# Three reorderings in a two-block transformer kernel on one core: sums of squares behind both chains, values' transposes ahead of the last tiles, output weights in idle buffers

## The chip, the cores and the metric

The kernel runs on one core of one Trainium2 chip. The metric is the device time of one launch in microseconds (us). PE is the matmul engine, DVE the vector engine, ACT the scalar engine, POOL GpSimd, SP the engine that issues the weights' DMAs. "PE waits for X" means that PE's next matmul needed a semaphore that X's last instruction raised.

## What is computed

512 tokens of width 1024 pass through two blocks of two layers each, all in float32. The first block's layer is feed-forward, token mixer, feed-forward; the second's, on 16 meta tokens and the 512, is token mixer, feed-forward. Cut to what matters:

```python
def first_block(x, ...):                       # per layer l
    x = x + 0.5 * rmsnorm(swiglu(rmsnorm(x, g1), w_gate, w_up, w_down), g2)
    x = x + rmsnorm(token_mixing(rmsnorm(x, g3), w_in, ..., w_out), g4)
    x = x + 0.5 * rmsnorm(swiglu(rmsnorm(x, g5), ...), g6)

def second_block(x, meta, ...):                # per layer l
    z = rms_norm(h, pre_g) @ w_in              # q, k, v, forget logits, conv parts
    y = concat([forgetting_attention(q, k, v, log_f), y_conv, y_sc])
    h = h + rms_norm(head_rms_norm(y, head_g) @ w_out, post_g)
    u = causal_depthwise_conv(rms_norm(h, g) @ w_up, conv_w)
    h = h + rms_norm((silu(gate) * up) @ w_down, post_g)
```

The first block's mixer ("mixer 1", M1) has three kinds of attention heads, of which one (stick-breaking) needs cumulative sums; the second's ("mixer 2", M2) is attention with a forget gate beside two convolutions.

## The kernel before, in words

**Stages.** The kernel is ten stages in a row, in the order F1 M1 F1 F1 M1 F1 M2 F2 M2 F2 (F for feed-forward, the digit for the block). Activations lie transposed: `x` is 128 partitions by 8 column groups by tokens. An edge is what lies between two stages: the last output columns of one, the residual sum, and the norm of the next. Tokens are cut into two halves h = 0 and 1 of about 256, so that an edge's work on one half runs beside matmuls of the other.

**Split floats.** Float32 products are made of three matmuls of a faster type: hi by hi, lo by hi, hi by lo. Weights come by DMA into two raw buffers, in granules of 128 x 1024 (512 KB). ACT writes a granule's hi part (`split_hi`, L589), DVE or POOL its lo part, raw minus hi (`split_lo`, L596; POOL in the mixers, DVE in the feed-forward stages). A "tile" is the three matmuls L605 to L607 or L646 to L648 (once for each half of the tokens where a stage has halves). `xhi`/`xlo` are the same parts of `x` (ACT L750, DVE L763). Each raw buffer is loaded again once both parts of its granule are made.

**An edge.** Each engine runs its own program in order; semaphores tie them. For each half, `dve_edge` scales the output (L851), adds it to `x` (L859), makes `xlo` (L763), and at the end `dve_x_sum` adds up the squares of the new `x` (L775, L777), which ACT has written into `y` (`act_x_square`, L755). Half 1's chain comes behind half 0's sum. `pe_first` runs the first three granules of the next stage piece by piece as `xhi`/`xlo` come; `pe_pre_sum` (L668) turns the DVE sum into the sum over all 1024 columns by one matmul, and ACT makes the norm factor `r` from it (L732, L734). `r` is applied to the outputs of the matmuls, so matmuls need only `xhi` and `xlo`, not `r`.

**Mixers.** In M1 and M2 PE walks through a list of steps: scores of one unit, transposes of the probabilities of an earlier one (`ptrans`), their product with the values (`pv`), and between them three parts of projection tiles (`st.parts`, `fill`) that need nothing of the attention. Some steps end with `vtrans`: four or five transposes of the values into PSUM, which ACT copies to `m_v` (L1542 in M1, L2103 in M2). The next step begins with a transpose into the same PSUM bank, which waits for that copy.

**The end of M2.** Output weights are 8 granules (OUT+0 to OUT+7; `OUT2_ORDER`, `omm`), for four pairs of output columns m = 0 to 3. m = 0 and 1 use the working buffers `whi`/`wlo`, m = 2 and 3 (`LATE`) buffers of their own (`m_late`). ACT's `act_out` makes the hi parts and moves the finished sums out of PSUM (`act_yevac`, L809 and L813); m = 3 of the matmuls waits for the PSUM banks of m = 1 (L646 waits for L813).

Of the kernel before, what the change touches and what calls it, by code (L numbers as in the profile page):

```python
# [316 lines left out]
def program(nc, I, out):  # L317
    with ExitStack() as ctx:
# [746 lines left out]

        def act_out(act, b, g, gb, gb2, qs, first=2):
# [5 lines left out]
            def hi_split(j):  # L1072
                m, q = divmod(j, nq)
                into = home(g, m, q)[0]
                n = qs[q] * PAIR
                if m not in LATE[g]:
                    split_hi(act, b, gb + j, gb2 + j // 2, j % 2, n)
                    return
                if KIND[g][0] == "F":
                    act.wait_ge(b.s.granules_done, gb + nq * late + {0: -1, 1: 0, 2: 1, 3: 1, 4: 2, 5: 2}[q] + CR)  # L1080
                elif m == late and q == 0:
                    act.wait_ge(b.s.pv_done, (LAYER[g] + 1) * (UNITS1 if b.n == 1 else UNITS2))
                split_hi(act, b, gb + j, gb2 + j // 2, j % 2, n, into)
# [1560 lines left out]
```

## Time and profile before

| what | value |
|---|---|
| median of 3 runs | 3505.8 us (3505.73 to 3506.83) |
| the profiled execution | 3504.3 us, its span 3502.6 us |
| granted clock of PE, mean | 0.992 of full |
| PE busy | 3376.0 us, 96% of the span |
| DVE, ACT, POOL busy | 1743.6, 1415.1, 312.5 us |

The span is the profiled part of the execution; 1.7 us of it lie around it. The busy time of PE is the modelled time of its matmuls, so that what is left for a schedule to win is PE's waits and the stretches at half clock.

### The profile page before, as it was taken

What the parts mean: (1) busy time and instruction counts of PE and PEld (TensorE: products, weight loads), DVE (VectorE), ACT (ScalarE), POOL (GpSimd) and SP (SyncE); (2) the same over time, 40 slices, a digit from 0 to 9 for tenths busy, and PEclk for the clock granted to TensorE, in tenths of its full rate; (3) what the DMA queues carried; (4) which work ended last, traced back from release to release, by engine and by line L of the source; (5) the groups of instructions that cost most, each with busy time, mean ns of one, the idle gap of its engine ahead of it and who ended that gap; (6) DMA issues with size and microseconds to landing.
All of it is one profiled execution on the core that took longest, in us unless ns stands there. A gap on an engine that the chain in (4) does not pass through costs nothing.

```text
span 3502.6 us, 52761 instructions
## 1 busy us (share of the span) xinstructions
PE 3376.0 (96%) x21254; PEld 2941.2 (84%) x21254; DVE 1743.6 (50%) x2382; ACT 1415.1 (40%) x2394; POOL 312.5 (9%) x167
## 2 busy tenths in 40 slices
PE   8999999899999999999899999988999999899998
PEld 7887866788888888866788889878999988789998
DVE  5442556544425442556544426735665366356643
ACT  4322445433234322445433234565443344644332
POOL 0000122100000000122000002210000022100000
PEclk9999999999999999999999999999999999999999
DMA  4343311233332332321233332212222321122222
GB/s 120 91 128 96 100 55 55 61 87 93 93 106 79 96 96 90 97 59 51 61 90 96 93 100 67 55 40 73 90 90 93 100 61 46 43 78 91 90 90 85
DMA packets 330446, 287.45 MB, mean 82 GB/s; under 512 B 9665, under 2 KB 326169, under 8 KB 330293
## 3 DMA queue, kind: packets, MB, share of 16 engines
q1 hardware_dynamic: 329348, 283.90, 27.2%
q8 instruction: 114, 1.87, 0.2%
q10 hardware_dynamic: 945, 1.37, 0.1%
q14 instruction: 39, 0.32, 0.0%
HBM read 283.10 MB, written 5.27 MB: 82 GB/s over the span
## 4 chain that ended last, share of the span: by engine, by line
PE 88%; DVE 5%; ACT 4%; issue 1%; DMA 1%; SPq 0%; ACTq 0%; DVEq 0%
PE ps L605 21%; PE ps L606 21%; PE ps L607 21%; PE ps L646 3%; PE ps L647 3%; PE ps L648 3%; PE ps L1783 2%; PE ps L1785 1%; PE ps L1784 1%; PE ps L698 1%; PE ps L1376 1%; PE ps L1400 1%; PE ps L1415 1%; PE ps L702 1%; PE ps L1832 1%
## 5 line engine op out<-in xcount | busy, mean ns | idle before, releaser
L605 PE MATMUL ps<-xhi,whi 128*128 128x512 f32 (+2 forms) x3088 | 1064.0, 345 | 4.1 <-DVE m_aconv L2170 4.0
L606 PE MATMUL ps<-xlo,whi 128*128 128x512 f32 (+2 forms) x3088 | 1057.3, 342 | 0.0
L607 PE MATMUL ps<-xhi,wlo 128*128 128x512 f32 (+2 forms) x3088 | 1053.1, 341 | 0.0
L596 DVE TENSOR_TENSOR wlo<-raw,whi 128x1024 fp32r<-128x1024 f32 x404 | 487.6, 1207 | 1114.3 <-ACT whi L589 1111.8
L589 ACT ACTIVATE whi<-raw 128x1024 fp32r<-128x1024 f32 (+1 forms) x495 | 515.4, 1041 | 1177.8 <-PE ps L607 1063.4
L605 PEld LDWEIGHTS ps<-xhi,whi 128*128 128x128 f32 x3088 | 583.4, 189 | 91.4 <-issue 19.0
L607 PEld LDWEIGHTS ps<-xhi,wlo 128*128 128x128 f32 x3088 | 582.4, 189 | 69.7
L606 PEld LDWEIGHTS ps<-xlo,whi 128*128 128x128 f32 x3088 | 582.9, 189 | 66.3 <-issue 0.5
L605 PE MATMUL ps<-hhi,whi 128*128 128x512 f32 (+2 forms) x1056 | 359.0, 340 | 0.9 <-issue 0.9
L606 PE MATMUL ps<-hlo,whi 128*128 128x512 f32 (+2 forms) x1056 | 358.1, 339 | 0.0
L607 PE MATMUL ps<-hhi,wlo 128*128 128x512 f32 (+2 forms) x1056 | 357.8, 339 | 0.0
L596 POOL TENSOR_TENSOR wlo<-raw,whi 128x1024 fp32r<-128x1024 f32 (+1 forms) x91 | 229.2, 2519 | 775.4 <-ACT whi L589 775.4
L782 POOL TENSOR_TENSOR S<-S 128x512 f32<-128x512 f32 (+5 forms) x58 | 77.8, 1341 | 2332.0 <-ACT S L809 2280.8
L605 PEld LDWEIGHTS ps<-hhi,whi 128*128 128x128 f32 x1056 | 198.9, 188 | 26.0 <-issue 2.7
L607 PEld LDWEIGHTS ps<-hhi,wlo 128*128 128x128 f32 x1056 | 198.6, 188 | 24.4
L606 PEld LDWEIGHTS ps<-hlo,whi 128*128 128x128 f32 x1056 | 198.9, 188 | 22.8
L1783 PE MATMUL ps<-xhi,whi 128*128 128x264 f32 x480 | 143.1, 298 | 1.9 <-DVE m_vt L2170 1.1
L1163 DVE SCALAR_TENSOR_TENSOR S<-S,par 128x528 f32<-128x528 f32 (+1 forms) x176 | 126.3, 759 | 24.1 <-ACT S L1027 18.2
L1043 ACT ACTIVATE hhi<-S 128x512 f32 (+4 forms) x132 | 82.3, 636 | 135.1 <-DVE S L1202 135.1
L1785 PE MATMUL ps<-xhi,wlo 128*128 128x264 f32 x480 | 136.3, 284 | 0.0
L1784 PE MATMUL ps<-xlo,whi 128*128 128x264 f32 x480 | 136.2, 284 | 0.0
L1035 ACT ACTIVATE S<-S 128x512 f32<-128x512 f32 (+2 forms) x132 | 82.0, 636 | 115.4 <-DVE S L1178 75.8
(274 smaller groups left out, 5150.9 us busy)
## 6 DMA issues: line engine op xcount, KB each, us to landing
raw<-in_ffn_w_up_dram SPq DMA_DIRECT2D x176, 512.0 KB, 3.7
raw<-in_ffn_w_down_dram SPq DMA_DIRECT2D x120, 512.0 KB, 3.4
raw<-in_w_in_dram SPq DMA_DIRECT2D x94, 512.0 KB, 3.8
raw<-in_ffn_w_gate_dram SPq DMA_DIRECT2D x88, 512.0 KB, 3.7
raw<-in_w_out_dram SPq DMA_DIRECT2D x32, 512.0 KB, 3.4
raw<-in_ffn_w_down_dram SPq DMA_DIRECT2D x24, 256.0 KB, 2.7
tbias_scratch<-rev_scratch SPq DMA_DIRECT2D x1, 3072.0 KB
y<-tbias_scratch SPq DMA_DIRECT2D x6, 512.0 KB, 6.1
```

Of the source, the lines that this page charges most:

```text
L589: act.activation(into[:, 0:n], raw[slot][:, 0:n], ACT.Copy).then_inc(b.s.weights_hi, 1)
L596: eng.tensor_tensor(lo[:, 0:n], raw[slot][:, 0:n], hi[:, 0:n].bitcast(F32), ALU.subtract).then_inc(b.s.weights_split, 1)
L605: pe.matmul(o, wh, hi[:, t0:t0 + w], start=first, stop=False)
L606: pe.matmul(o, wh, lo[:, t0:t0 + w], start=False, stop=False)
L607: ins = pe.matmul(o, wl, hi[:, t0:t0 + w], start=False, stop=last)
L646: pe.matmul(o, wh, hi, start=first, stop=False)
L647: pe.matmul(o, wh, lo, start=False, stop=False)
L648: return pe.matmul(o, wl, hi, start=False, stop=last)
L1163: ins = dve.scalar_tensor_tensor(out=c_, in0=S[o][:, k:k + b.T], scalar=tap(l, k, 2 * i + o, up), in1=c_, op0=ALU.mult, op1=ALU.add)
L1783: pe.matmul(o, wh, xhi[:, t, t0:t0 + w], start=(t == 0), stop=False)
L1784: pe.matmul(o, wh, xlo[:, t, t0:t0 + w], start=False, stop=False)
L1785: ins = pe.matmul(o, wl, xhi[:, t, t0:t0 + w], start=False, stop=(t == 7))
```

## The change

It has three parts, which share no semaphore and can be read one by one.

1. **Sums behind both chains.** In `dve_edge` the two calls of `dve_x_sum` stand behind both halves' chains. ACT's last squares stand one `xhi` later. In `pe_first` the two `pe_pre_sum` stand behind the first and the second half of granule 2's tiles of h = 1. Where more tiles of the stage's start follow (F2's `rest`, M2's fourth granule), each half waits for its own norm.
2. **Values' transposes ahead of the last tiles.** In steps with a `vtrans`, M1 and M2 call it before `fill(st.parts[2])` and not behind it. M1's step 0 runs all its tiles ahead of its scores.
3. **Output weights of m = 1 in idle buffers.** OUT+2 is split into `whi[2]`/`wlo[2]` in step 20 and OUT+3 into `ahi`/`alo` (a convolution's, free by then) in step 21, by ACT and DVE; OUT+4 and OUT+5 ahead of m = 0's evacuation. The output tiles k = 1 and 2 of m = 0 move from behind the steps into steps 21 and 22. `m_late` of M2 moves to another place in memory.

```diff
+OUT_STEP = {20: 2, 21: 3}
...
-    steps[21].parts = [[], [], [("o", 0, 6), ("o", 1, 6)]]
-    steps[22].parts = [[], [("o", 0, 4), ("o", 1, 4)], [("o", 0, 5), ("o", 1, 5)]]
+    steps[21].parts = [[], [("o", 0, 1), ("o", 1, 1)], [("o", 0, 6), ("o", 1, 6)]]
+    steps[22].parts = [[("o", 0, 2), ("o", 1, 2)], [("o", 0, 4), ("o", 1, 4)], [("o", 0, 5), ("o", 1, 5)]]
...
         def home(g, m, q):
+            if KIND[g] == "M2" and m == 1:
+                if q == 0:
+                    return whi[2], wlo[2]
+                return [t[:, :, :].rearrange("p a t -> p (a t)")[:, 0:1024] for t in (m2.ahi, m2.alo)]
...
-                else:
-                    pe_pre_sum(pe, g, 0)
                 half = len(tiles[2]) // 2
                 for t in tiles[2][:half]:
                     tile(h, 2, t)
                 if h == 1:
-                    pe_pre_sum(pe, g, 1)
+                    pe_pre_sum(pe, g, 0)
                 for t in tiles[2][half:]:
                     ins = tile(h, 2, t)
-            if rest:
-                pe.wait_ge(e.norm_log, pre(g, 1))
+                if h == 1:
+                    pe_pre_sum(pe, g, 1)
+            for h in range(2):
+                if rest:
+                    pe.wait_ge(e.norm_log, pre(g, h))
                 for t in rest:
-                    for h in range(2):
-                        ins = tile(h, 2, t)
+                    ins = tile(h, 2, t)
...
                 if nxt is not None:
                     dve_x_lo(dve, g + 1, nxt, h, 3)
+            if nxt is not None:
+                for h in range(2):
                     dve_x_sum(dve, g + 1, h, ch)
...
+        def out_hi(act, b, g, gb, gb2, qs, j):
+            nq, late = len(qs), LATE[g][0]
+            m, q = divmod(j, nq)
+            into = home(g, m, q)[0]
+            n = qs[q] * PAIR
+            if m not in LATE[g] and not (KIND[g] == "M2" and m == 1):
+                split_hi(act, b, gb + j, gb2 + j // 2, j % 2, n)
+                return
+            if KIND[g][0] == "F":
+                act.wait_ge(b.s.granules_done, gb + nq * late + {0: -1, 1: 0, 2: 1, 3: 1, 4: 2, 5: 2}[q] + CR)
+            elif m == 1:
+                act.wait_ge(b.s.granules_done, gb - (1 - q) + CR)
+            elif m == late and q == 0:
+                act.wait_ge(b.s.pv_done, (LAYER[g] + 1) * (UNITS1 if b.n == 1 else UNITS2))
+            split_hi(act, b, gb + j, gb2 + j // 2, j % 2, n, into)
...
+                if j == 0 and KIND[g] == "M2":
+                    for i in range(nq * late, nq * late + 2):
+                        hi_split(i)
                 if j == nq * late - 1 and KIND[g][0] == "M":
-                    for i in range(nq * late, nq * DOWN_PAIRS):
+                    for i in range(nq * late + (2 if KIND[g] == "M2" else 0), nq * DOWN_PAIRS):
                         hi_split(i)
                     next_hi(0)
...
-                fill(st.parts[2])
                 if st.vt is not None:
                     vtrans(st.vt)
+                if st.sc != 0:
+                    fill(st.parts[2])
...
+                if n_step in OUT_STEP:
+                    out_hi(act, b, sub, g2b(l) + OUT2, g2b2(l) + OUT2 // 2, OUT_Q, OUT_STEP[n_step])
...
-            for k in (1, 2):
-                for o in range(2):
-                    otile(o, k)
```

**DVE at an edge.** DVE's rows of the edge into the first mixer, before: the sum of half 0 (rows two to four) stands between half 0's last `xlo` and half 1's chain.

```order
L763 SCALAR_TENSOR_TENSOR xlo<-x,par,xhi 128x256 x4
L775 TENSOR_TENSOR y<-y 128x4x256
L775 TENSOR_TENSOR y<-y 128x2x256
L777 TENSOR_TENSOR y<-y 128x256
L851 SCALAR_TENSOR_TENSOR S<-y,S 128x512
L859 TENSOR_TENSOR x<-x,S 128x2x256
L851 SCALAR_TENSOR_TENSOR S<-y,S 128x512
```

The same place after the change:

```order
L768 SCALAR_TENSOR_TENSOR xlo<-x,par,xhi 128x256 x2
L864 TENSOR_TENSOR x<-x,S 128x2x256
L768 SCALAR_TENSOR_TENSOR xlo<-x,par,xhi 128x256 x4
L780 TENSOR_TENSOR y<-y 128x4x256
L780 TENSOR_TENSOR y<-y 128x2x256
L782 TENSOR_TENSOR y<-y 128x256
L780 TENSOR_TENSOR y<-y 128x4x256
L780 TENSOR_TENSOR y<-y 128x2x256
L782 TENSOR_TENSOR y<-y 128x256
```

The six sum rows now stand together behind the last `xlo`, ahead of nothing but the stage's own work; half 1's first L856 (L851 of before) follows directly on half 0's last `xlo`.

**PE at a values' transpose.** PE's rows at the end of an M1 step with `vtrans` (`m_vt`), before: all tiles, then the transposes, then the next step's first transpose (`m_w`) into the same bank.

```order
L607 MATMUL ps<-xhi,wlo 128x512
L605 MATMUL ps<-xhi,whi 128x512
L606 MATMUL ps<-xlo,whi 128x512
L607 MATMUL ps<-xhi,wlo 128x512
L1391 MATMUL ps<-ident,m_vt 128x128 x4
L1400 MATMUL ps<-ident,m_w 128x128
L1376 MATMUL ps<-m_k,m_q 128x384 x2
```

And after:

```order
L1410 MATMUL ps<-ident,m_vt 128x128 x4
L605 MATMUL ps<-xhi,whi 128x512
L606 MATMUL ps<-xlo,whi 128x512
L607 MATMUL ps<-xhi,wlo 128x512
L605 MATMUL ps<-xhi,whi 128x512
L606 MATMUL ps<-xlo,whi 128x512
L607 MATMUL ps<-xhi,wlo 128x512
L1419 MATMUL ps<-ident,m_w 128x128
```

Two tiles (six matmuls) now stand between the transposes of the values and the next transpose.

**ACT at the end of M2.** ACT's rows from the head norm's last operation to the evacuation of m = 1, before; the first row of L589 is OUT+2 and OUT+3.

```order
L2077 ACTIVATE m_ohi<-y,par 128x528
L589 ACTIVATE whi<-raw 128x1024 x2
L809 ACTIVATE S<-ps 128x528 x2
L813 ACTIVATE y<-ps,par 128x528 x2
L1093 ACT_TABLE_LOAD
L589 ACTIVATE m_late<-raw 128x1024 x4
L589 ACTIVATE whi<-raw 128x1024
L809 ACTIVATE S<-ps 128x528 x2
L813 ACTIVATE y<-ps,par 128x528 x2
```

And after (`m_ahi` stood in step 21, some rows ahead of this piece, `whi[2]` in step 20):

```order
L2105 ACTIVATE m_ohi<-y,par 128x528
L590 ACTIVATE m_late<-raw 128x1024 x2
L814 ACTIVATE S<-ps 128x528 x2
L818 ACTIVATE y<-ps,par 128x528 x2
L1107 ACT_TABLE_LOAD
L590 ACTIVATE m_late<-raw 128x1024 x2
L590 ACTIVATE whi<-raw 128x1024
L814 ACTIVATE S<-ps 128x528 x2
L818 ACTIVATE y<-ps,par 128x528 x2
```

Between the two evacuations (L809/L813, now L814/L818) stand two late splits and one of the next stage, where there were four and one; ahead of the first stand the other two.

## Rows read from the trace of the kernel before

**Rows 1.** The page, part 1, busy time of PE.
```profile
PE 3376.0 (96%) x21254; PEld 2941.2 (84%) x21254; DVE 1743.6 (50%) x2382; ACT 1415.1 (40%) x2394; POOL 312.5 (9%) x167
```

**Rows 2.** The waits of PE: us in total, times, longest.
```profile
PE ps L1400 <- ACT m_v L1542: 12.6, 16, 0.9
...
PE ps L1870 <- ACT m_v L2103: 7.4, 8, 0.9
...
PE ps L605 <- DVE m_aconv L2170: 4.0, 2, 2.0
```

**Rows 3.** The timeline of PE into the first mixer: start, us, what, [idle before].
```profile
402.62 0.36 PE L698 MATMUL ps<-xhi,whi 128*128 128x256 f32 x1 [1.20 <-ACT xhi L750]
...
411.56 0.59 PE L668 MATMUL ps<-y,ones 128*128 128x256 f32 x2
...
413.63 0.50 PE L605 MATMUL ps<-xhi,whi 128*128 128x512 f32 x1
```

**Rows 4.** The waits of PE at that edge, 400 to 414 us.
```profile
PE ps L702 <- DVE xlo L763: 0.8, 2, 0.5
```

**Rows 5.** The timeline of ACT at the same edge.
```profile
396.30 0.42 ACT L734 ACTIVATE S<-S 128x256 f32<-128x256 f32 x1
```

**Rows 6.** The timeline of DVE at the same edge.
```profile
399.78 0.43 DVE L777 TENSOR_TENSOR y<-y 128x256 f32<-128x256 f32 x1
400.12 0.69 DVE L851 SCALAR_TENSOR_TENSOR S<-y,S 128x512 f32<-128x512 f32 x1
...
408.63 1.95 DVE L775 TENSOR_TENSOR y<-y 128x1024 f32<-128x1024 f32 x2
```

**Rows 7.** The timeline of POOL at the same edge.
```profile
411.18 2.40 POOL L596 TENSOR_TENSOR wlo<-raw,whi 128x1024 fp32r<-128x1024 f32 x1 [47.11 <-ACT whi L589]
```

**Rows 8.** DVE beside POOL in mixer 2, first alone, then overlapped.
```profile
2218.07 2.12 DVE L2219 SCALAR_TENSOR_TENSOR m_aconv<-m_apad,par,m_aconv 128x528 f32<-128x528 f32 x3
...
2221.99 2.42 DVE L2219 SCALAR_TENSOR_TENSOR m_aconv<-m_apad,par,m_aconv 128x528 f32<-128x528 f32 x2
```

**Rows 9.** The timeline of POOL in the same stretch.
```profile
2220.77 2.40 POOL L596 TENSOR_TENSOR wlo<-raw,whi 128x1024 fp32r<-128x1024 f32 x1 [14.09 <-ACT whi L589]
```

**Rows 10.** The timeline of DVE, edge from mixer 1 to feed-forward.
```profile
708.52 1.23 DVE L596 TENSOR_TENSOR wlo<-raw,whi 128x1024 fp32r<-128x1024 f32 x1
```

**Rows 11.** PE at the same edge, first matmul of the last granule there.
```profile
710.85 0.28 PE L646 MATMUL ps<-xhi,whi 128*128 128x256 f32 x1
```

**Rows 12.** PE at the edge from mixer 2 to feed-forward.
```profile
2420.01 0.56 PE L698 MATMUL ps<-xhi,whi 128*128 128x264 f32 x1 [2.62 <-ACT xhi L750]
```

**Rows 13.** PE at the values' transposes of unit 4, mixer 1.
```profile
449.76 0.39 PE L607 MATMUL ps<-xhi,wlo 128*128 128x512 f32 x1
449.99 0.60 PE L1391 MATMUL ps<-ident,m_vt 128*128 128x128 f32 x4
451.37 0.30 PE L1400 MATMUL ps<-ident,m_w 128*128 128x128 f32 x1 [0.78 <-ACT m_v L1542]
```

**Rows 14.** ACT at the values' transposes of unit 24, mixer 1.
```profile
596.40 0.60 ACT L1485 ACTIVATE m_pt<-ps 128x512 f32<-128x512 f32 x1 [0.17 <-ACT m_w L1516]
```

**Rows 15.** The waits of PE, 2345 to 2390 us, end of mixer 2.
```profile
PE ps L646 <- ACT y L813: 5.5, 1, 5.5
PE ps L605 <- DVE wlo L596: 3.4, 2, 2.5
PE ps L605 <- DVE m_olo L2273: 1.6, 1, 1.6
```

**Rows 16.** ACT at the end of mixer 2.
```profile
2384.07 1.06 ACT L589 ACTIVATE whi<-raw 128x1024 fp32r<-128x1024 f32 x1 [2.81 <-DMA raw<-in_ffn_w_up_dram]
...
2386.01 1.29 ACT L813 ACTIVATE y<-ps,par 128x528 f32<-128x528 f32 x2
```

**Rows 17.** Windows: PE, PEld, DVE, ACT, POOL busy, granted clock, DMA share, GB/s.
```profile
2385.45:2392.28 6.83, 4.92 (x22) 4.92 (x23) 3.88 (x3) 5.05 (x10) 3.71 (x3) 0.50 0.39 117
2143.10:2146.50 3.40, 3.40 (x18) 3.40 (x17) 1.57 (x2) 0.00 (x0) 0.30 (x1) 0.50 0.78 222
```

More of the change, by code:

```diff
@@ L1072, in hi_split @@
             def hi_split(j):
[L1073 to L1083, printed above, removed]
+                out_hi(act, b, g, gb, gb2, qs, j)
             def next_hi(j):
@@ L1130, in act_out @@
                 act_x_square(act, g + 1, 0, p)
-            for p in range(4):
+            act_x_hi(act, g + 1, nxt, 1, 0)
+            for p in range(1, 4):
                 act_x_hi(act, g + 1, nxt, 1, p)
-                act_x_square(act, g + 1, 1, p)
+                act_x_square(act, g + 1, 1, p - 1)
+            act_x_square(act, g + 1, 1, 3)
         def first_hi(act, g, j):
@@ L1433, in pe_mix1 @@
                 if st.sc == 0:
-                    fill(st.parts[0])
+                    for part in st.parts:
+                        fill(part)
                 if st.sc is not None:
@@ L1442, in pe_mix1 @@
                     ptrans(u, 1)
-                fill(st.parts[1])
+                if st.sc != 0:
+                    fill(st.parts[1])
                 if st.extra is not None:
                     norm_sums(0)
-                fill(st.parts[2])
                 if st.vt is not None:
                     vtrans(st.vt)
+                if st.sc != 0:
+                    fill(st.parts[2])
                 if st.extra is not None:
@@ L1536, in act_mix1 @@
                     outputs(p_)
-                for g in st.done_in[1] + st.done_in[2]:
+                for g in st.done_in[1]:
                     if g < 24:
@@ L1543, in act_mix1 @@
                                    ACT.Copy).then_inc(s.transposed_out, 1)
+                for g in st.done_in[2]:
+                    if g < 24:
+                        hi_split(g + 2)
                 if st.extra is not None:
@@ L1803, in omm @@
                 wcol = (k % 4) * PAIR + o * P
-                return tile_mm(pe, b, obank(sub, m, o), j, wcol, m2.ohi[:, k, :], m2.olo[:, k, :], first, last)
+                return tile_mm(pe, b, obank(sub, m, o), j if m == 0 else home(sub, m, j), wcol, m2.ohi[:, k, :],
+                               m2.olo[:, k, :], first, last)
             def otile(o, k):
@@ L1920, in pe_mix2 @@
             pe_first(pe, b, sub, g2b(l), [[(gbank(g), t * P, t, t == 0, t == 7) for t in range(8)] for g in range(3)])
-            for g in range(3, 8):
+            pe.wait_ge(s.weights_split, g2b(l) + 3 + 1 + CR)
+            for h, (t0, w) in enumerate(halves(b)):
+                pe.wait_ge(e.norm_log, pre(sub, h))
+                for t in range(8):
+                    ins = part_mm(pe, ps[:, gbank(3) + h, 0:w], whi[1][:, t * P:t * P + P], wlo[1][:, t * P:t * P + P],
+                                  xhi[:, t, t0:t0 + w], xlo[:, t, t0:t0 + w], t == 0, t == 7)
+            ins.then_inc(s.granules_done, 1)
+            for g in range(4, 8):
                 for t in range(8):
@@ L1939, in pe_mix2 @@
                     sums(st.sums[1], n_step)
-                fill(st.parts[2])
                 if st.vt is not None:
                     vtrans(st.vt, n_step)
+                fill(st.parts[2])
                 if st.sums[2] is not None:
@@ L2316, in dve_mix2 @@
                     mul(c)
+                if n_step in OUT_STEP:
+                    j = OUT_STEP[n_step]
+                    hi_, lo_ = home(sub, 1, j % 2)
+                    split_lo(dve, b, g2b(l) + OUT2 + j, j % 2, hi=hi_, lo=lo_)
                 for c in LO_STEP.get(n_step, ()):
```

11 lines of the change are left out of this document (5 added, 6 removed).

## The prediction, made blind

> **What bounds the kernel now.** I read the page's busy times first, then PE's waits, then the timeline at each kind of place the change touches. PE is busy for 3376.0 of 3502.6 us [rows 1], so no other engine's load matters by itself; only PE's waits and its stretches at half clock can be won. Part 1 of the change aims at the waits at the edges ([rows 3, 4, 12] show two kinds), part 2 at the 16 and 8 waits for `m_v`, 12.6 and 7.4 us in all [rows 2], part 3 at the end of mixer 2, where the longest wait is L646's for ACT's L813, 5.5 us [rows 15].
>
> All sums are in the clock of the profiled execution, 3504.3 us; the median of the runs is 1.5 us above it, and I add that at the end. Less than 0.2% (7 us) counts as no change.
>
> **Part 1, the edges.** There are nine: two into M1, three into F1, two into M2, two into F2.
>
> The chain of half 1 on DVE starts at 400.12, when half 0's sum ends (L777 from 399.78, 0.43 long) [rows 6]. Its own input, the norm factor of half 1, was ready at 396.30 + 0.42 = 396.72 [rows 5]. So it can start 3.4 us earlier. PE's waits there are 1.20 us for `xhi` [rows 3] and 0.8 us for `xlo` [rows 4], together 2.0; the first matmul after a wait is longer too (0.36 us against 0.28 [rows 3, 11]), and for the three restarts I put 0.8, an estimate. The most that an edge can give is thus 2.8, the least 2.0, before what is late next.
>
> Late next are the sums. Both now follow the last `xlo`. One takes 1.95 + 0.43 = 2.4 us [rows 6]. Before, half 1's sum began at 408.63; now the last `xlo` ends at 408.63 - 3.4 = 405.2, and half 1's sum runs from 407.6 to 410.0, where it ended at 411.0. It is 1.0 us earlier, not 3.4. What that does differs by kind of edge:
>
> *Into F1.* DVE's lo split of the fourth granule was made at 708.52, 1.23 long, behind one sum [rows 10]. Behind two it starts at 708.52 - 3.4 + 2.4 = 707.5 and ends at 708.7. PE would come to that granule at 710.85 - 2.8 = 708.1 [rows 11]. A wait of 0.6 to 0.7 comes back: gain 2.1 each, 6.3 in three. Bounds: 2.8 if the split isn't needed that soon, 1.0 (all bound by the sums).
>
> *Into M1.* The lo split there is POOL's. It began at 411.18, 2.40 long [rows 7], when ACT's hi part was done and half 1's sum as well. ACT's hi part follows PE's progress, so POOL now wants to start near 408.4, in the middle of half 1's sum. In mixer 2 three L2219 take 2.12 us, 0.71 each; the two that start while POOL's split runs from 2220.77 to 2223.17 take 2.42, and the second ends 1.2 us after POOL does [rows 8, 9]. So one was held until POOL ended, 1.0 us longer than alone. By this the rest of the sum (L777, or half of L775 and L777) ends with POOL or after it: POOL from 409.0 to 411.4, the sum at 411.8 to 412.4. PE wants it for `pe_pre_sum` at about 411.56 + 1.6 - 2.8 = 410.4 (1.6 for the four tiles that it moves behind; with its own matmul they are what lies between 411.56 and 413.63). That is a wait of 1.4 to 2.0, and the edge gives 1.1, not 2.8: 2.2 in two. Bounds: 2.8 and 0.4 each.
>
> The Trainium skill, "SBUF — State Buffer", "Who interferes with whom", says that a DVE instruction with two SBUF inputs and a GpSimd instruction share a port pair that the earlier one holds to its end. The trace's held L2219 agrees; without the rule an overlap would cost nothing, and the edges would give 2.8.
>
> *Into M2.* The same overlap with POOL. Behind it PE is bound by a chain that starts with `r`: PE waits 2.0 us for `m_aconv` at each of the two [rows 2], which comes from `r`. Without a hold `r` is 1.0 to 1.2 us earlier and so is PE; held, it is 0.2 to 0.9 later. I take -0.4 each, -0.8 in two; bounds +1.2 and -0.9. PE arrives earlier at that wait, so it grows to 3.7 us or more; the stretch at half clock that follows it already (2143.10, 3.4 us at 0.50 [rows 17], thus 1.7 us) may grow as much again: a bound of -1.7 each, left out of the sum.
>
> *Into F2.* PE waits 2.62 [rows 12]. As at F1, DVE's split and the sums take some back; I take 2.0 each, 4.0 in two; bounds 3.5 (the slower matmuls behind it won too) and 1.0.
>
> Part 1: 2.2 + 6.3 - 0.8 + 4.0 = **11.7**.
>
> **Part 2, values' transposes.** The four transposes start at 449.99 and the next at 451.37, after 0.78 idle [rows 13]. With two tiles between them, six matmuls or 1.4 us (0.23 each, from L607 at 449.76 to the next start), ACT's copy is covered. So each place can give about 0.85 with the restart, if the transposes can start where they are now put. They need the PSUM bank that ACT's copy of the step's second transposes of probabilities (L1485) frees. That copy had those two tiles as cover and loses it. For units 4 to 16 the copy ends early enough. At unit 24 it starts at 596.40 and ends at 597.00 [rows 14], where PE wants it at 595.7, two tiles ahead of before: there PE idles for 1.3 more, the later cover gives 0.8 back, a loss of 0.5. Unit 20 gives 0.5; unit 0 is bound by its own chain and unit 28 has no third part of tiles: nothing. Per layer 4 x 0.85 + 0.5 - 0.5 = 3.4, in two 6.8. Bounds: 12.6 (all) and -3.
>
> M2's eight waits are 7.4 us, 0.93 each [rows 2]. The three later ones of a layer give 0.95 to 1.0, the first 0.55, since DVE's chain to the next scores is nearly as long: 3.5 a layer, 7.0 in two. Bounds 8.8 and 3.
>
> Part 2: **13.8**.
>
> **Part 3, the end of mixer 2.** From 2345 to 2390 PE waits 5.5 + 3.4 + 1.6 = 10.5 us [rows 15], and 6.83 us run at half clock with 4.92 busy [rows 17], 2.4 lost: 12.9 a layer. The 3.4 (two lo splits, of OUT+2 and OUT+3) go, since those are now made in steps 20 and 21, in buffers of their own. The 5.5: ACT's evacuation of m = 1 stands behind five hi splits that wait for DMAs (the last 2.81 us [rows 16]), and ends at 2386.01 + 1.29 = 2387.30. Two of the five move ahead of the first evacuation, and all raw buffers come free earlier. I keep 1.5 of the 5.5. Against this, each added split takes 1.06 us of ACT [rows 16] and 1.23 of DVE [rows 10] in steps 20 and 21, ahead of copies for which PE waits: 1.0 more for the transposes of unit 19, and the wait for `m_olo` becomes 1.8. Left: 1.5 + 1.0 + 1.8 = 4.3 of 10.5. With waits below 2 us no half clock: the gain is 10.5 - 4.3 + 2.4 = 8.6, taken as 8.5, 17.0 in two. Bounds: if the evacuation stays late, 3.4 + 1.6 - 2.8 = 2.2; if its wait goes altogether, 10.
>
> What moves past other work: ACT's added splits wait for raw buffers; SP's loads follow in the same order as before. No DMA is added.
>
> **Sum.** 11.7 + 13.8 + 17.0 = 42.5. 3504.3 - 42.5 = 3461.8, and with 1.5 for the median **3463 us** (-1.2%).
>
> **The rivals.**
>
> *No hold between DVE and POOL at the edges.* The overlap costs nothing: 2 x 1.7 more into M1, 2 x 1.6 into M2, 6.6 in all: 3457. For it: two L775 of three may slip in ahead of POOL. Against: [rows 8, 9].
>
> *The evacuation of m = 1 stays the last.* Part 3 gives 2.2 a layer instead of 8.5: 3463 + 12.6 = 3476. For it: all the splits there waited for DMAs, and the last two still do. Against: their buffers come free some 7 us earlier.
>
> *Slower: the values' transposes wait for ACT's copy everywhere, as at unit 24.* If the copy ends more than 0.5 us after PE's two-tile point in all 22 places with a cover, each costs 0.5 instead of giving 0.6 on the mean, and the idle time, then near 2 us, can bring a stretch at half clock with it, 1.7 us (3.4 at 0.50, [rows 17]). 22 x (0.5 + 1.7) = 48 against the 28.7 of the other parts: 3505.8 + 20 = 3525. It decides from 1.3 us a place. For it: unit 24. Against: only there do table loads stand ahead of the copy.
>
> *Almost nothing comes:* the waits only move (the mixers' chains of DVE are as long as PE's tiles): about 3502.
>
> **How the numbers follow.** My forecast's case 0.53, no hold 0.20, late evacuation 0.17, almost nothing 0.05, slower 0.05 (some of it within 0.2%). The likeliest gives 3463. The range holds the first three cases: down to 3457 less 9 for the upper bounds of F1, F2 and parts 2 and 3, up to 3476 with 6 for half clock behind the two waits in M2 and the lower bounds of part 2: **3448 to 3482**. Faster 0.93, within 0.2% 0.04, slower 0.03.
>
> **What would show it.** Right: half 1's `xhi` wait at the first M1 edge gone; `pe_pre_sum` of half 1 waiting 1.4 to 2.0 there and a DVE sum row longer than before beside POOL's; 0.6 of wait for L597 into F1; no wait behind `m_v` for units 4 to 16, but one before the transposes of unit 24; the wait for ACT's L818 near 1.5 with the clock whole behind it. Wrong: sums of unchanged length beside POOL, a wait for L818 of 5 us, waits of over 0.5 us before the transposes in most steps, or new half-clock stretches behind the edges into M2.

## The result, and the profile after

The changed kernel takes 3470.2 us (median of 4 runs, 3468.33 to 3471.96) against 3506.3 us (3505.73 to 3507.27) for the kernel before: ratio 0.9898, 95% interval 0.9886 to 0.991, so 36 us or 1.0% faster. Forecast were 3463, with 3448 to 3482 as the range. The profiled execution is the slowest of the four (3471.96, span 3470.2), so the traces differ by 32.4 us. Where experiments are set beside the changed kernel below, the medians and the spread of the runs are compared. The interval of the ratio of e8 and of e10 lies wholly below that of the changed kernel; those of e4, e5, e6, e7 and e9 (about 0.3% wide) overlap with it. The kernel before itself had medians from 3505.3 to 3506.7 beside the different groups of runs, so a difference of some 1.5 us between groups says little.

The page, part 1, and the waits of PE (us in total, times, longest) of the changed kernel:

```profile
PE 3369.2 (97%) x21254; PEld 2937.3 (85%) x21254; DVE 1756.2 (51%) x2382; ACT 1414.8 (41%) x2394; POOL 311.8 (9%) x167
```

```profile
PE ps L673 <- DVE y L782: 9.4, 8, 1.7
...
PE ps L605 <- DVE m_aconv L2200: 7.2, 2, 3.6
...
PE ps L1806 <- DVE m_vt L2218: 5.0, 4, 2.1
PE ps L1410 <- ACT m_pt L1507: 3.9, 4, 1.7
...
PE ps L1419 <- ACT m_v L1564: 3.0, 4, 0.8
```

Against [rows 2]: of the 16 waits for M1's `m_v` (12.6 us) four are left (3.0), the eight for M2's are gone. Grown or new are the four waits before M1's values' transposes (3.9 in all, where there were two of 0.3), eight for the sums of squares (9.4), and in each M2 two for `m_vt` L2218, of 2.1 and 0.4, where there was one of 0.4. The wait for `m_aconv` has grown from 2.0 to 3.6 each.

The gain by stage, read as the difference of the start times of the same matmul (the first of the norm's sums, L659, now L664, at a stage's end) in the two traces:

| stage | forecast | measured |
|---|---|---|
| ahead of the first M1 | 0 | -1.6 |
| M1, each of two | 4.5 (edge 1.1, transposes 3.4) | 4.2 and 5.4 |
| F1, each of three | 2.1 | 2.1, 2.1, 2.1 |
| M2, each of two | 11.6 (-0.4, 3.5, 8.5) | 7.5 and 6.6 |
| F2, each of two | 2.0 | 1.9 and 2.0 |

The first row is no work of the change: PE waited 1.89 us once at 268 us, where the change touches nothing, against 0.90 in the kernel before, which is 1.0 of the 1.6. Everything else that is missing from the forecast is in M2.

**The edge into M1.** The timelines of DVE, POOL and PE there (start, us, engine, line, what, [idle before <- released by]), which answer to [rows 3], [rows 6] and [rows 7]:

```profile
408.89 0.42 DVE L782 TENSOR_TENSOR y<-y 128x256 f32<-128x256 f32 x1
409.23 4.00 DVE L780 TENSOR_TENSOR y<-y 128x1024 f32<-128x1024 f32 x2
413.27 0.43 DVE L782 TENSOR_TENSOR y<-y 128x256 f32<-128x256 f32 x1
```

```profile
410.05 2.63 POOL L597 TENSOR_TENSOR wlo<-raw,whi 128x1024 fp32r<-128x1024 f32 x1 [44.36 <-ACT whi L590]
```

```profile
413.75 0.48 PE L673 MATMUL ps<-y,ones 128*128 128x256 f32 x1 [1.73 <-DVE y L782]
```

Half 0's sum takes 1.9 + 0.4; of half 1's, two L780 take 4.00 together where they took 1.95. POOL's split starts at 410.05 and ends at 412.68 (410.05 + 2.63), inside them. The wait for `xhi` is gone, and one of 1.73 for half 1's sum has come.

**Mixer 2.** PE at its beginning and at unit 0's transposes, and windows (PE, PEld, DVE, ACT, POOL busy, granted clock, DMA share, GB/s), which answer to [rows 17]:

```profile
2117.87 0.71 PE L673 MATMUL ps<-y,ones 128*128 128x264 f32 x2 [1.50 <-DVE y L782]
...
2128.03 0.56 PE L605 MATMUL ps<-xhi,whi 128*128 128x264 f32 x1 [3.62 <-DVE m_aconv L2200]
```

```profile
2180.55 0.36 PE L1806 MATMUL ps<-xhi,whi 128*128 128x264 f32 x1 [2.09 <-DVE m_vt L2218]
```

```profile
2127.50:2134.50 7.00, 6.46 (x30) 6.50 (x31) 3.05 (x4) 0.91 (x2) 1.81 (x1) 0.53 0.55 150
2181.50:2185.00 3.50, 3.50 (x18) 2.08 (x16) 3.45 (x3) 0.54 (x3) 2.13 (x1) 0.56 0.06 9
2364.00:2371.00 7.00, 5.44 (x45) 5.23 (x44) 3.03 (x2) 4.69 (x7) 3.17 (x2) 1.00 0.44 140
3021.50:3025.00 3.50, 3.50 (x18) 3.50 (x18) 1.70 (x3) 0.76 (x2) 0.00 (x0) 0.52 0.50 150
```

Behind the longer wait for `m_aconv` 7.0 us now run at a mean clock of 0.53, where the kernel before had 3.4 us at 0.50. There is a second stretch, behind a wait of 2.09 that was 0.40 (at 2192.50 in the kernel before). The one at the end of the first M2 is gone: the third window, around the wait for L818, has the full clock. In the second M2 one stretch is left near the end (the fourth window), behind a wait for `m_olo` of 1.54.

**The end of mixer 2.** The waits of PE there in the first M2, against [rows 15]:

```profile
PE ps L651 <- ACT y L818: 1.6, 1, 1.6
PE ps L605 <- DVE m_olo L2303: 1.5, 1, 1.5
PE ps L1896 <- ACT m_pt L2041: 1.4, 1, 1.4
```

From 10.5 us of waits 4.5 are left, where 4.3 were forecast.

### The profile page after: what moved, and what is told of

It is laid out like the page before. It is cut to its first block, busy times and chain, and to the rows that moved or that the text cites. A ratio compares the mean times of both kernels' runs of the same rounds, so it can differ in the third digit from the quotient of the medians.

```text
span 3470.2 us, 52759 instructions
## 1 busy us (share of the span) xinstructions
PE 3369.2 (97%) x21254; PEld 2937.3 (85%) x21254; DVE 1756.2 (51%) x2382; ACT 1414.8 (41%) x2394; POOL 311.8 (9%) x167
## 4 chain that ended last, share of the span: by engine, by line
PE 86%; DVE 8%; ACT 4%; DMA 1%; issue 1%; SPq 0%; ACTq 0%; DVEq 0%
PE ps L605 22%; PE ps L606 21%; PE ps L607 21%; PE ps L651 3%; PE ps L652 3%; PE ps L653 3%; PE ps L1806 1%; PE ps L1808 1%; PE ps L1807 1%; DVE m_aconv L2249 1%; DVE y L780 1%; PE ps L1395 1%; PE ps L1419 1%; PE ps L1434 1%; DVE x L864 1%
## 5 line engine op out<-in xcount | busy, mean ns | idle before, releaser
L597 DVE TENSOR_TENSOR wlo<-raw,whi 128x1024 fp32r<-128x1024 f32 (+1 forms) x402 | 485.2, 1207 | 1099.4 <-ACT whi L590 1096.8
L597 POOL TENSOR_TENSOR wlo<-raw,whi 128x1024 fp32r<-128x1024 f32 (+1 forms) x91 | 228.6, 2513 | 768.1 <-ACT whi L590 768.1
```

Of the source, the lines that this page charges most:

```text
L597: eng.tensor_tensor(lo[:, 0:n], raw[slot][:, 0:n], hi[:, 0:n].bitcast(F32), ALU.subtract).then_inc(b.s.weights_split, 1)
```

## The experiments

The kernel before ran beside all of them on the same chip: median 3505.5 us beside the first four, 3505.3 beside the next four, 3506.7 beside the last two.

### Each part by itself

**e1.** The kernel before with part 1 alone (the hunks of `dve_edge`, `pe_first`, ACT's squares and the per-half waits):

```diff
                 if nxt is not None:
                     dve_x_lo(dve, g + 1, nxt, h, 3)
+            if nxt is not None:
+                for h in range(2):
                     dve_x_sum(dve, g + 1, h, ch)
...
                 for t in tiles[2][:half]:
                     tile(h, 2, t)
                 if h == 1:
-                    pe_pre_sum(pe, g, 1)
+                    pe_pre_sum(pe, g, 0)
```

> Part 1 alone on the kernel before. By the terms as the changed kernel's trace corrects them: 2.2 into M1, 6.3 into F1, -0.8 and two longer half-clock stretches (-3.4) into M2, 4.0 into F2: 8.3 us faster, 3498. Theory X (the 2.1 us wait for m_vt at mixer 2's first unit belongs to part 2, which brings PE to DVE's chain sooner): here that wait stays at 0.4 (2192.50 in the kernel before). Rival Y (it belongs to part 1: r comes later and POOL's splits overlap other DVE work): the wait is about 2 us here too, with a half-clock stretch behind it, and the gain is 5 to 6 us less, about 3 us. Half 1's sum (L775 of before) held by POOL to about 4.0 us at both kinds of mixer edge under either.

Measured: 3497.6 us (3496.48 to 3500.92, 10 runs), ratio 0.9976 (0.9966 to 0.9986), 7.9 us faster. The timeline of PE:

```profile
412.45 0.70 PE L668 MATMUL ps<-y,ones 128*128 128x256 f32 x2 [1.73 <-DVE y L777]
...
415.49 0.49 PE L1380 MATMUL ps<-m_k,m_q 64*128 64x128 f32 x4 [0.94 <-DVE m_k L1576]
```

```profile
2189.21 0.36 PE L1785 MATMUL ps<-xhi,whi 128*128 128x264 f32 x1 [0.41 <-DVE m_vt L2197]
```

The wait for `m_vt` at M2's unit 0 is 0.41: part 1 does not make it, and rival Y falls. Half 1's sum is held (L775 takes 4.00 here too). Behind the wait for the sum stands another, 0.94 for `m_k`, which the changed kernel doesn't show. The two longer half-clock stretches into M2 that were expected did not come: behind the same wait for `m_aconv` (3.6) each M2 has one stretch of 3.4 us, as the kernel before.

**e2.** The kernel before with part 2 alone:

```diff
-                fill(st.parts[2])
                 if st.vt is not None:
                     vtrans(st.vt)
+                if st.sc != 0:
+                    fill(st.parts[2])
```

In M1 this part also puts ACT's last hi splits of a step behind its copy of `m_v`.

> Part 2 alone on the kernel before. Mixer 1: 3.4 a layer, 6.8. Mixer 2: units 1 to 3 give 3.2 a layer. Theory X: unit 0 costs 2.9 a layer (the wait for m_vt grows from 0.4 to 2, half clock behind it), so 0.3 a layer: 7.4 us in all, 3499. Rival Y: unit 0 gives its 0.55, 3.7 a layer: 14.2 us, 3492. The slower case (ACT's copy late everywhere) would show waits of over 0.5 us before the values' transposes at most units; expected at units 20 (0.3) and 24 (1.7) alone.

Measured: 3497.5 us (3495.18 to 3500.44, 10 runs), ratio 0.9976 (0.9967 to 0.9986), 8.0 us faster, as theory X has it. The timeline of PE at M2's unit 0:

```profile
2188.00 0.36 PE L1789 MATMUL ps<-xhi,whi 128*128 128x264 f32 x1 [2.09 <-DVE m_vt L2194]
```

**e3.** The kernel before with part 3 alone (`OUT_STEP`, `home`, `out_hi`, the moved output tiles):

```diff
+                if n_step in OUT_STEP:
+                    out_hi(act, b, sub, g2b(l) + OUT2, g2b2(l) + OUT2 // 2, OUT_Q, OUT_STEP[n_step])
```

> Part 3 alone on the kernel before: 8.8 a layer as in the changed kernel, 17.6 us, 3489; the wait for ACT's m = 1 evacuation 1.4 to 1.6 instead of 5.5 and no half clock behind it. Rival (it only works with what part 1 and 2 free): the wait stays over 3 us, 5 to 10 us in all.

Measured: 3490.4 us (3487.80 to 3492.04, 4 runs), ratio 0.9955 (0.9938 to 0.9972), 15 us faster. The waits of PE at the end of mixer 2:

```profile
PE ps L651 <- ACT y L818: 1.7, 1, 1.7
PE ps L605 <- DVE m_olo L2288: 1.6, 1, 1.6
PE ps L1888 <- ACT m_pt L2026: 1.4, 1, 1.4
```

They are those of the changed kernel, so part 3 takes the waits away by itself. By stage M2 gains 6.6 and 7.5 us here. The clock did not do all that was expected: in the first M2 3.4 us at half clock stand behind the wait of 1.7 for L818 (2383.5 to 2386.9), the stretch at 2318 is longer, and one at 2346 is new, so that this stage has as much time at half clock as in the kernel before; the second M2 has one stretch less.

The three parts alone add up to 31 us, all together give 36. By stage, e1 loses 1.1 us in each M1, with one half-clock stretch more in each than the kernel before (1.7 us), and e2 gains 3.0 and 3.3 there.

In the traces 3.4 of these 5 us lie at the beginning of M1, where parts 1 and 2 help each other. From the stage's start (L659) to the same matmul behind unit 0 (at 440.0 and 1484.0 in the kernel before), e1 gains 0.2 and 0.1 us, e2 0.0 and -0.4, the changed kernel 1.7 and 1.5: 3.4 us more than both, in the two layers together. In the first M1 e1 waits there 1.7 for the sum, 0.9 for `m_k` and 0.8 for `m_w`, e2 still 2.0 at the edge and then 1.3 for `m_v`, the changed kernel 1.7 for the sum and 0.7 for `m_v`. The rest is within the noise of the runs and of the half-clock stretches.

### The wait at mixer 2's unit 0

**e4.** The changed kernel with unit 0's transposes back behind the tiles:

```diff
-                if st.vt is not None:
+                if st.vt is not None and st.vt != 0:
                     vtrans(st.vt, n_step)
                 fill(st.parts[2])
+                if st.vt == 0:
+                    vtrans(st.vt, n_step)
```

> The changed kernel with mixer 2's unit 0 transposes again behind the step's last tiles; units 1 to 3 and mixer 1 stay moved. Theory X: its wait for m_vt returns to 0.4, no half clock there, but the 0.93 wait for ACT's copy of m_v is back: 2.9 to 3.5 a layer faster than the changed kernel, 6 to 7 us, 3464. Rival Y: the wait for m_vt stays at about 2 us, plus 0.93: 0 to 2 us slower than the changed kernel, 3470 to 3472.

Measured: 3467.5 us (3466.80 to 3470.14), ratio 0.9894 (0.9877 to 0.991), by the medians 2.7 us faster than the changed kernel, less than the 6 to 7 expected, and not clear of the noise. PE's timeline shows both waits at their old size:

```profile
2168.19 0.27 PE L1894 MATMUL ps<-ident,m_w 128*32 128x128 f32 x1 [0.93 <-ACT m_v L2133]
...
2180.41 0.36 PE L1806 MATMUL ps<-xhi,whi 128*128 128x264 f32 x1 [0.39 <-DVE m_vt L2220]
```

The runs overlap (the changed kernel's begin at 3468.33). In the trace the two M2 stages gain 9.9 and 10.6 us over the kernel before, where they gained 7.5 and 6.6 in the changed kernel. Not all of that is unit 0's: behind the wait for `m_aconv`, which is 3.6 in both, e4 has one stretch at half clock in each M2 and the changed kernel two, 1.2 to 1.4 us a layer. Across unit 0 alone, by the start times of the same matmuls, e4 loses nothing against the kernel before and the changed kernel 2.2 and 2.1.

What lies ahead of the 2.09 is in DVE's and POOL's timelines, from DVE's first `m_k` of the step to `m_vt`. The changed kernel:

```profile
2166.09 0.43 DVE L2218 TENSOR_TENSOR m_k<-ps,r 128x264 f32<-128x264 f32 x1 [2.46 <-PE ps L1808]
2166.44 4.32 DVE L2249 SCALAR_TENSOR_TENSOR m_aconv<-m_apad,par,m_aconv 128x528 f32<-128x528 f32 x3
...
2171.38 1.43 DVE L2249 SCALAR_TENSOR_TENSOR m_aconv<-m_apad,par,m_aconv 128x528 f32<-128x528 f32 x2
...
2179.97 0.77 DVE L2218 TENSOR_TENSOR m_vt<-ps,r 128x264 f32<-128x264 f32 x2
```

```profile
2167.14 2.38 POOL L597 TENSOR_TENSOR wlo<-raw,whi 128x1024 fp32r<-128x1024 f32 x1 [9.24 <-ACT whi L590]
```

The kernel before:

```profile
2178.11 0.43 DVE L2188 TENSOR_TENSOR m_k<-ps,r 128x264 f32<-128x264 f32 x1 [1.93 <-PE ps L1785]
2178.46 2.12 DVE L2219 SCALAR_TENSOR_TENSOR m_aconv<-m_apad,par,m_aconv 128x528 f32<-128x528 f32 x3
...
2181.74 0.72 DVE L2264 TENSOR_REDUCE m_nmax<-ps 128x2 f32<-128x544 f32 x1 [1.09 <-PE ps L1842]
2182.38 2.42 DVE L2219 SCALAR_TENSOR_TENSOR m_aconv<-m_apad,par,m_aconv 128x528 f32<-128x528 f32 x2
...
2191.92 0.77 DVE L2188 TENSOR_TENSOR m_vt<-ps,r 128x264 f32<-128x264 f32 x2
```

Three L2249 take 4.32 in the changed kernel where three L2219 took 2.12, with POOL's split from 2167.14 to 2169.52 in them. POOL starts when ACT's hi part is made, and ACT makes that directly behind its copy of `m_v`, which the change brought forward. In the kernel before the same split came 1.5 us later against the work around it and held the next two operations instead, by 1.0 (2.42 for 1.43). So the hold grew by 1.2 us, and it took what PE's earlier scores had freed, DVE's idle 1.09: the chain from `m_k` to `m_vt` is 13.8 us long before (2178.11 to 2191.92) and 13.9 after (2166.09 to 2179.97). It also starts 0.5 later against its surroundings, because the tile whose result `m_k` takes now stands behind the transposes: DVE's idle ahead of `m_k` is 2.46 for 1.93, and 1.94 in e4. PE, 1.1 earlier because it no longer waits for `m_v`, meets an `m_vt` that is 0.6 later: the 0.40 becomes 2.09.

**e9.** The changed kernel, unit 0's transposes left ahead of the tiles, and that one split of POOL made to wait for those three DVE operations:

```diff
             for g in range(3, SPLIT2_DVE):
+                if g == 10:
+                    pool.wait_ge(b2.s.dw_taps, l * len(DW_OPS) + 2 * DW_PER_STEP)
```

> The changed kernel, with POOL's split of granule 10 of mixer 2 (the one that starts at 2167.14 in the changed kernel, inside three L2249 of DVE) waiting until DVE's first ten convolution operations are done. Unit 0's transposes stay ahead of the step's last tiles. Theory: the hold is the whole cause of the 2.09 wait for m_vt; the three L2249 take 2.1 again instead of 4.3, the wait shrinks to 0.4 to 0.9 with no half-clock stretch behind it, 3 us a layer: 3464 to 3466. Rival: the chain of DVE is the bound there in any case (as the prediction had it, with 0.55 to gain), and POOL's later split is waited for: 3468 to 3471.

Measured: 3466.9 us (3465.76 to 3469.55), ratio 0.989 (0.9874 to 0.9907), 3.4 us under the changed kernel's median, the runs overlapping by one. DVE, POOL and PE:

```profile
2165.56 2.12 DVE L2249 SCALAR_TENSOR_TENSOR m_aconv<-m_apad,par,m_aconv 128x528 f32<-128x528 f32 x3
...
2168.29 5.31 DVE L2249 SCALAR_TENSOR_TENSOR m_aconv<-m_apad,par,m_aconv 128x528 f32<-128x528 f32 x2
```

```profile
2167.76 2.39 POOL L597 TENSOR_TENSOR wlo<-raw,whi 128x1024 fp32r<-128x1024 f32 x1 [10.74 <-DVE m_aconv L2249]
2170.64 2.39 POOL L597 TENSOR_TENSOR wlo<-raw,whi 128x1024 fp32r<-128x1024 f32 x1 [0.49 <-ACT whi L590]
```

```profile
2170.20 0.39 PE L1806 MATMUL ps<-xhi,whi 128*128 128x264 f32 x1 [0.79 <-POOL wlo L597]
...
2179.20 0.36 PE L1806 MATMUL ps<-xhi,whi 128*128 128x264 f32 x1 [0.55 <-DVE m_vt L2218]
```

The three take 2.12 again, but the hold is moved and not gone: the next two L2249 take 5.31 where they took 1.43, beside this split and the one behind it, and the chain from `m_k` to `m_vt` is 13.4 us long (2165.21 to 2178.62) for 13.9. The wait for `m_vt` is 0.55, and 0.79 of wait for POOL's later split has come; together they are 1.34, what the kernel before waited here (0.93 and 0.40). Neither wait has a half-clock stretch behind it. Across unit 0 e9 loses 0.2 us against the kernel before, where the changed kernel loses 2.2. So both theory and rival of the expectation came in part, and what e9 wins is mostly the stretch. "The hold is the whole cause" is not shown: no run has this chain without a hold.

### The edges into the mixers

**e5.** The changed kernel with POOL's split of the fourth granule behind both sums:

```diff
+                if g == 3:
+                    pool.wait_ge(e.x_summed, 2 * (l * 3 + 1) + 2)
```

> The changed kernel, with POOL's split of the fourth granule in both mixers waiting until both sums of squares are done, so that they can't overlap. If POOL holds DVE (theory H): the sum of half 1 takes 1.9 us again instead of 4.0 and ends 2.1 us earlier against the stage's start; into mixer 1 PE then waits 1 to 1.5 us for POOL's lo part instead of 1.7 for the sum (little changes), into mixer 2 the forget chain, and PE, come 2 us earlier: about 3 to 4 us faster than the changed kernel, 3467. Rival (the long sum has another cause, such as ACT's squares or a wait for y): the sum stays at 4.0 us and the kernel is 2 to 4 us slower, 3473, as POOL's part is now late too.

Measured: 3464.9 us (3463.16 to 3465.13), ratio 0.9884 (0.9868 to 0.9901), 5.3 us faster than the changed kernel. DVE and PE:

```profile
408.04 1.95 DVE L780 TENSOR_TENSOR y<-y 128x1024 f32<-128x1024 f32 x2
410.01 0.42 DVE L782 TENSOR_TENSOR y<-y 128x256 f32<-128x256 f32 x1
```

```profile
412.92 0.50 PE L605 MATMUL ps<-xhi,whi 128*128 128x512 f32 x1 [1.67 <-POOL wlo L597]
```

The sum is at 1.95 + 0.42 again with nothing changed but POOL's start. The kernel's slowest run is 3 us under the changed kernel's fastest. Into M1 PE waits as long as before the amendment, now for POOL (1.67), and the M1 stages gain 3.6 and 4.6 us over the kernel before, no more than the changed kernel's. The gain is in M2, 10.5 and 10.9 us for 7.5 and 6.6: the first wait for `m_aconv` is 1.94 instead of 3.62 and ends 1.7 us earlier (1.2 ahead of the kernel before and not 0.5 behind it). One stretch at half clock less stands behind it, too, but e4 has that as well, with a wait of 3.6, so it can't be put down to POOL's start.

**e6.** The changed kernel with that lo part made by DVE behind both sums, and POOL starting one granule later:

```diff
-            for g in range(3, 26):
-                split_lo(pool, b1, mgb(l) + g, g % 2, handover=(g == 3))
+            for g in range(4, 26):
+                split_lo(pool, b1, mgb(l) + g, g % 2, handover=(g == 4))
...
+            split_lo(dve, b, mgb(l) + 3, 1)
             dve.wait_ge(e.norm_made, pre(sub, 1))
```

The same stands in mixer 2.

> The changed kernel, with DVE and not POOL making the fourth granule's lo part in both mixers, behind both sums (as at the edges into feed-forward). Theory H: no overlap, both sums at 1.9 and 0.4 us, the lo part ready 1.2 us behind them: PE waits 0.4 to 0.6 there into mixer 1 instead of 1.7, and comes 2 us earlier into mixer 2's chain: 5 us faster than the changed kernel, 3465. Rival: DVE's longer queue delays the first evacuations in the mixers by 1.2 us and gives it all back: 3469 to 3471.

Measured: 3463.4 us (3458.41 to 3464.56), ratio 0.9877 (0.9861 to 0.9894), 6.8 us faster than the changed kernel. PE:

```profile
411.51 0.50 PE L605 MATMUL ps<-xhi,whi 128*128 128x512 f32 x1 [0.37 <-DVE wlo L597]
```

```profile
423.42 0.30 PE L1419 MATMUL ps<-ident,m_w 128*128 128x128 f32 x1 [1.76 <-ACT m_v L1564]
```

Of the 1.73 into M1 0.37 is left, but the wait for `m_v` at unit 0, 0.71 in the changed kernel, is 1.76: the chain from `r` to it hardly got shorter, so the M1 stages gain 4.3 and 5.9 for 4.2 and 5.4. In M2 it is 10.2 and 10.4; the wait for `m_aconv` ends 1.2 and 1.4 us ahead of the kernel before, as in e5. Unit 0's wait of 2.09 is there in both layers, and in the first no half clock follows it: the loss across unit 0 is then 0.6 and not 2.2, which gives the stretch's part as 1.6.

**e7.** The changed kernel with M1's step 0 as before, its scores behind the first third of the tiles:

```diff
                 if st.sc == 0:
-                    for part in st.parts:
-                        fill(part)
+                    fill(st.parts[0])
```

> The changed kernel with mixer 1's step 0 as before: scores(0) behind the first third of its tiles. Part 1 alone showed a wait of 0.94 us for m_k at those scores. Theory: the tiles ahead of scores(0) are what hides the later r in the changed kernel: the wait is back here and mixer 1 is 1 to 1.5 us slower a layer, 3472 to 3474. Rival: the wait for m_v at unit 0 (0.7) shrinks by as much, no difference, 3470.

Measured: 3470.2 us (3469.60 to 3471.06), ratio 0.9901 (0.9884 to 0.9917): no difference in the medians, the rival. The 0.94 for `m_k` is back, and the wait for `m_v` at unit 0, 0.71 in the changed kernel, is gone. In the traces the first matmul behind unit 0 comes 0.5 us later against the stage's start than in the changed kernel, in both layers, less than half of what the theory had and too little for the runs to show.

### Together

**e8.** e6, e4's amendment, and M1's unit 24 back behind its tiles:

```diff
-                if st.vt is not None:
+                if st.vt is not None and st.vt != 6:
                     vtrans(st.vt)
                 if st.sc != 0:
                     fill(st.parts[2])
+                if st.vt == 6:
+                    vtrans(st.vt)
```

> The changed kernel with three amendments: the fourth granule's lo part by DVE, mixer 2's unit 0 transposes and mixer 1's unit 24 transposes behind the step's last tiles as before. If the gains add (5 from the first, 3 from the second as measured, 1 from the third): 3461. If the first gives nothing: 3466.

Measured: 3458.6 us (3455.13 to 3460.10), ratio 0.9864 (0.9848 to 0.9881). At unit 24, the changed kernel and this one:

```profile
593.18 0.63 PE L1410 MATMUL ps<-ident,m_vt 128*128 128x128 f32 x4 [1.68 <-ACT m_pt L1507]
```

```profile
593.71 0.63 PE L1410 MATMUL ps<-ident,m_vt 128*128 128x128 f32 x4 [0.28 <-ACT m_pt L1509]
595.11 0.30 PE L1419 MATMUL ps<-ident,m_w 128*128 128x128 f32 x1 [0.78 <-ACT m_v L1566]
```

1.68 against 0.28 + 0.78: the loss forecast for unit 24 (0.5 a layer) was there, 0.6, and is taken back. The slowest run is 8 us under the changed kernel's fastest. The sum of the single gains, 3461, was 2 us too high.

**e10.** The same with e9's amendment in place of e4's:

```diff
+                if g == 10:
+                    pool.wait_ge(b2.s.dw_taps, l * len(DW_OPS) + 2 * DW_PER_STEP)
```

> The combined kernel (3458.6) with unit 0 of mixer 2 treated as in the run before it, ahead of the tiles and POOL waiting, and not put back behind them. If the wait of PE there is gone: 0.5 to 1 us a layer faster than the combined kernel, 3457, hardly to be told from it by the runs, but by the wait at unit 0. If POOL's wait doesn't help: 3463.

Measured: 3457.6 us (3456.87 to 3459.33), ratio 0.9863 (0.9847 to 0.988), as expected, and not to be told from e8. Both beat the changed kernel by about 12 us and the one before by 47 to 49.

## Why the prediction was right, and where it was off

The forecast was 7 us too low, within its range: 36 us of gain for 42.5. Its large terms came out each for the reason given, so this is not luck; one term had the wrong sign, and one premise about the clock did not hold. By its own steps:

- **Edges into F1 and F2.** Right: 2.1 and 1.9 to 2.0 a stage for 2.1 and 2.0. The wait for L597 was 0.41 at each F1 edge for the 0.6 forecast; at F2 the sums took their part back (0.49 and 0.94).
- **Edges into M1.** Right in mechanism and size: the two L780 were held, the sum ended 1.0 us after POOL's split did, and PE waited 1.73 for 1.4 to 2.0. At the first matmul of the fourth granule the edge had given 1.2 for 1.1. e5 and e6 show that the overlap and nothing else lengthens the sum, so the case "no hold" fell. What that case would give was wrong too: "the edges would give 2.8" without a hold. In e5 PE then waits for POOL's lo part (1.67), in e6 for the chain from `r` to unit 0 (1.76), and M1 gains 0 to 0.5 more at most. What bounds the edge next was not looked for behind the sums.
- **Edges into M2.** -0.5 for -0.4 up to the end of the wait for `m_aconv`, and without the hold +1.2 to +1.4 (e5, e6) for the bound of +1.2: right. The half-clock stretch, "left out of the sum" with a bound of -1.7 each, came in both M2 stages: 7.0 us at a mean of 0.53 for 3.4 at 0.50, and 1.2 us more lost (in the first M2 the gap between the two traces is 13.8 at the wait's end and 12.6 at 2168.11 and 2155.56). It was one of the prediction's own signs of being wrong. But it does not follow from the longer wait alone: e1 and e4, with the same 3.6, have one stretch there, as the kernel before.
- **M1's transposes.** 3.4 a layer forecast, 3.5 in each between units 4 and 24. The M1 stages gained 4.2 and 5.4 with the edge in it, for 4.5; unit 24 showed 1.68 of wait, unit 20 0.26. The 0.5 by which unit 0 gained, for which nothing was forecast, came from parts 1 and 2 together. The slower case, that the copy is late everywhere, fell: only those two show it.
- **M2's transposes: the step that failed.** "the first 0.55, since DVE's chain to the next scores is nearly as long". Unit 0 cost 2.2 a layer instead: 0.6 up to its wait's end (12.55 to 11.96 between the traces) and 1.6 in the half-clock stretch behind the wait. What the step left out is that the chain itself would move. It starts 0.5 later, behind the transposes, and it doesn't get the 1.1 us shorter that PE's earlier scores allow, since the moved copy of `m_v` lets ACT's next hi part, and so POOL's split, start inside three DVE operations, where it holds them for 2.2 us and not two later ones for 1.0. Without that growth of 1.2 `m_vt` would be 0.6 early and not 0.6 late, by this estimate from the two timelines, close to the 0.55. This is the mechanism of the edges, seen in [rows 8, 9] and applied to them alone. Units 1 to 3 gave 1.1 each at their transposes; at unit 1 the same thing took 0.7 back (three L2249 from 2208.29 take 4.31 for the 2.12 of [rows 8], and PE waits 0.43 for `m_vt` at 2222.37, where it waited for nothing before), so 2.6 for 2.95.
- **The end of mixer 2.** Right in the waits: 4.5 left for 4.3. The case of a late evacuation fell (e3). The premise "With waits below 2 us no half clock" held in the first M2 (8.8 for 8.5) and not in the second (7.4, with 3.4 us at half clock from 3021.6 behind a wait of 1.54); in e3 a wait of 1.7 has a stretch behind it. No row of the prediction showed it.

Of the 42.5 us forecast the traces lack 10.1: 1.6 ahead of the first M1 and 9.1 in the two M2 stages, with 0.6 more than forecast elsewhere. In the first M2 the 4.1 are the edge's stretch at half clock (1.2, and 0.1 at its wait), unit 0 (2.2, and 0.55 that didn't come) and units 1 to 3 (0.3), less 0.3 more than forecast at the end. In the second M2 the stretch near its end, which the first doesn't have, costs 1.4 of the 5.0.

Open stays what unit 0 of M2 would give with no hold at all in DVE's chain, and what decides whether a wait has one half-clock stretch behind it, two or none.

## What to carry to other kernels

When an operation moves, follow what it releases on every other engine, down to the lowest: here one copy moved 1.5 us ahead on ACT, POOL's split behind it then ran into other DVE operations than before and held them for longer, and PE paid with a wait and a slower clock. Where two engines hold each other up, it is worth making the one with slack wait (e5), or giving its work to the other at that one place (e6); look then at where the hold has gone, since in e9 it only moved to the next two operations. A wait that is forecast to grow to 2 us and more can cost nearly as much again in clock (1.6 behind 2.09), and that belongs into the sum with a chance of its own. Two parts of a change that share no semaphore can still need each other: at the beginning of M1 parts 1 and 2 gave next to nothing alone and 1.5 to 1.7 us together.

## What the runs showed of the hardware

- **DVE and POOL.** Where a DVE operation with two operands in SBUF met POOL's subtraction of two SBUF operands, one DVE operation was held until POOL ended: two L780 4.00 us for 1.95, three L2249 4.32 for 2.12. POOL's split, met by a DVE operation under way, took 2.63 for 2.40. In each of the twelve traces 20 of the 124 `m_aconv` operations of the two M2 stages are held, each beside a split of POOL, and none is long without one. The order of the work changes how long the holds are: the durations of the 124 add up to 128.8 us in the kernel before, 136.3 in the changed kernel, 133.7 in e4 and 135.4 in e9. The Trainium skill, "SBUF — State Buffer", "Who interferes with whom", says that a DVE instruction with two SBUF inputs contends with a GpSimd instruction that reads SBUF; the traces agree.
- **The clock after one and the same wait.** A wait of 4.48 us before L1400 stands in both M1 stages of the kernel before, with the same work behind it. The first was followed by one stretch at half clock, the second by twice as much. Windows of the kernel before:

```profile
620.50:624.50 4.00, 4.00 (x14) 2.50 (x13) 2.74 (x7) 1.68 (x3) 0.00 (x0) 0.57 0.00 0
1665.00:1672.50 7.50, 5.52 (x22) 3.50 (x24) 5.80 (x12) 1.68 (x3) 0.00 (x0) 0.54 0.06 21
```

  Two windows of the changed kernel, at the same two waits, both long:

```profile
615.00:622.50 7.50, 5.71 (x24) 3.69 (x26) 5.80 (x12) 1.68 (x3) 0.00 (x0) 0.54 0.03 9
1652.50:1660.00 7.50, 4.77 (x14) 3.04 (x14) 5.83 (x11) 1.68 (x3) 0.00 (x0) 0.54 0.17 58
```

  So a wait's price in clock differs by up to 1.7 us without a cause that the traces show, and a stage's gain in one pair of traces carries that much noise. Corrected for the first M1's longer stretch, it gained up to 5.9 and not 4.2, and the second 5.4. The wait for `m_aconv` shows it best, since it stands twice in each of the twelve traces, with the same work behind it:

| wait | traces | us at half clock behind it, each of the two |
|---|---|---|
| 1.8 to 2.0 | before, e2, e5 | 3.4 and 3.4 in all three |
| 2.0 | e3 | none and 3.4 |
| 3.1 to 3.2 | e8 | 3.4 and 3.4 |
| 3.1 to 3.2 | e6, e10 | none and 3.4 in both |
| 3.6 | e1, e4 | 3.4 and 3.4 in both |
| 3.6 | e9 | 3.4 and 6.8 |
| 3.6 | changed kernel, e7 | 6.8 and 6.8 in both |

  Only waits of 3.6 had 6.8 us behind them, five of ten. Within one trace the two layers mostly agree, so they are not independent draws.
